# Fourth layer of a four-layer transformer kernel: the order of one division on VectorE, and the forget weights as 32 standing columns

## What is computed

```python
kvf = hs @ shared_w_kvf                       # hs: normed rows, 256 x 1024
k_sh = rms_norm(split_heads(kvf[..., :HD]), shared_k_norm_g)
f_logit = kvf[..., 2 * HD:] + shared_b_f      # 16 columns, one per head
f_cum = lax.cumsum(jax.nn.log_sigmoid(f_logit), axis=1).transpose(0, 2, 1)
q = rms_norm(split_heads(hn @ fox_w_q[j]), fox_q_norm_g[j])
...
logits = einsum('bhqd,bhkd->bhqk', qb, k) * scale + fb[..., :, None] - f_cum[:, :, None, :]
logits = jnp.where(causal, logits, -jnp.inf)
probs = jax.nn.softmax(logits, axis=-1)       # per tile of 128 queries
out = einsum('bhqk,bhkd->bhqd', probs, v)
```

## Time and profile before

| | before |
|---|---|
| median of 3 runs (lowest, highest) | 1344.83 us (1344.74, 1345.34) |
| the profiled execution's own time | 1345.62 us |
| its span, first to last instruction | 1343.5 us |
| PE busy, share of the span | 1327.1 us, 99% |
| PEld busy | 1104.4 us, 82% |
| DVE busy | 920.0 us, 68% |
| ACT busy | 779.2 us, 58% |
| POOL busy | 109.4 us, 8% |
| granted TensorE clock | 1.000 |
| HBM | 238.33 MB read, 178 GB/s over the span |

### The profile page before, as it was taken

How to read it: one execution, slowest core, us unless ns; L and a number is a source line. 1 busy time by engine, 2 the same in 40 slices (tenths; PEclk the granted TensorE clock), 3 DMA queues, 4 the chain that set the end, 5 groups by cost and what they waited for, 6 DMA issues and landing times.

```text
span 1343.5 us, 20709 instructions
## 1 busy us (share of the span) xinstructions
PE 1327.1 (99%) x6866; PEld 1104.4 (82%) x6866; DVE 920.0 (68%) x1612; ACT 779.2 (58%) x1415; POOL 109.4 (8%) x175
## 2 busy tenths in 40 slices
PE   8999999999999999999999999999999999999998
PEld 6987888888898788888888888888887778888887
DVE  6887665656787765555688875555677887655565
ACT  7666555546765655554675565555477766555544
POOL 4031232300000000000010000000002210000000
PEclk9999999999999999999999999999999999999999
DMA  8444777765554455555644455656645545655551
GB/s 315 150 157 134 213 221 219 219 205 182 181 165 142 146 183 187 187 187 187 213 140 152 131 172 188 187 187 187 203 157 181 167 133 164 195 187 187 187 200 51
DMA packets 144863, 240.32 MB, mean 179 GB/s; under 512 B 12643, under 2 KB 103314, under 8 KB 144801
## 3 DMA queue, kind: packets, MB, share of 16 engines
q1 hardware_dynamic: 141648, 230.41, 53.2%
q0 software_dynamic: 2832, 8.49, 3.2%
q10 hardware_dynamic: 320, 0.60, 0.1%
HBM read 238.33 MB, written 1.13 MB: 178 GB/s over the span
## 4 chain that ended last, share of the span: by engine, by line
PE 91%; DVE 5%; DMA 1%; ACT 1%; issue 1%; POOL 0%; SPq 0%; DVEq 0%
PE acc L1442 14%; PE acc L1444 14%; PE acc L1443 14%; PE sc L1444 11%; PE sc L1442 11%; PE sc L1443 11%; PE turn L1603 5%; PE acc L1553 3%; PE acc L1555 2%; PE acc L1554 2%; DVE wlo L1022 2%; PE turn L1690 1%; DMA raw<-in_qk 1%; PE sc L1650 1%; PE sc L1645 1%
## 5 line engine op out<-in xcount | busy, mean ns | idle before, releaser
L1022 DVE SCALAR_TENSOR_TENSOR wlo<-raw,gain,whi 128x512 fp32r<-128x512 f32 (+2 forms) x612 | 429.6, 756 | 26.3 <-ACT whi L735 26.3
L735 ACT ACTIVATE whi<-raw,gain 128x512 fp32r<-128x512 f32 (+2 forms) x612 | 404.5, 721 | 32.3 <-PE acc L1444 23.4
L1442 PE MATMUL sc<-whi,xhi 128*128 128x512 f32 x640 | 252.9, 395 | 0.0
L1444 PE MATMUL sc<-whi,xlo 128*128 128x512 f32 x640 | 249.7, 390 | 0.0
L1443 PE MATMUL sc<-wlo,xhi 128*128 128x512 f32 x640 | 249.3, 389 | 0.0
L1442 PE MATMUL acc<-whi,xhi 128*128 128x512 f32 x432 | 173.4, 401 | 3.2 <-DVE wlo L1033 1.8
L1444 PE MATMUL acc<-whi,xlo 128*128 128x512 f32 x432 | 168.7, 390 | 0.0
L1443 PE MATMUL acc<-wlo,xhi 128*128 128x512 f32 x432 | 168.4, 390 | 0.0
L1020 DVE TENSOR_TENSOR wlo<-raw,whi 128x1024 fp32r<-128x1024 f32 x120 | 141.8, 1217 | 0.0
L1444 PEld LDWEIGHTS sc<-whi,xlo 128*128 128x128 f32 x640 | 120.1, 188 | 25.6
L1443 PEld LDWEIGHTS sc<-wlo,xhi 128*128 128x128 f32 x640 | 120.3, 188 | 24.0
(11 more groups left out here) (194 smaller groups left out, 1992.3 us busy)
## 6 DMA issues: line engine op xcount, KB each, us to landing
raw<-in_ffn_w_gu SPq DMA_DIRECT2D x176, 256.0 KB
raw<-in_qk SPq DMA_DIRECT2D x62, 512.0 KB
raw<-in_ffn_w_gate SPq DMA_DIRECT2D x88, 256.0 KB
raw<-in_ffn_w_up SPq DMA_DIRECT2D x88, 256.0 KB
raw<-in_ffn_w_down SPq DMA_DIRECT2D x44, 512.0 KB
raw<-in_ffn_w_d SPq DMA_DIRECT2D x44, 512.0 KB
raw<-in_ple_w_gate SPq DMA_DIRECT2D x32, 512.0 KB
raw<-in_da_w_qkv SPq DMA_DIRECT2D x8, 512.0 KB
```

What stands on the lines that cost most here:

```text
L735: ins = act.activation(whi[:, u % RING, c0:c1], raw[:, u % RING, c0:c1], ACT.Copy, scale=scale)
L1022: ins = dve.scalar_tensor_tensor(out=lo, in0=w, scalar=gain[:, g:g + 1], in1=hi.bitcast(F32), op0=ALU.mult, op1=ALU.subtract)
L1442: pe.matmul(dst, xh, wh, start=first, stop=False)
L1444: return pe.matmul(dst, xl, wh, start=False, stop=last)
```

## The change

Two edits, both in the fourth layer.

1. In `DVE_STEPS` the entry r = 4 of L_FX is written the other way round: `post0`, the division of tile 0, comes ahead of `scores1`, the maxima of tile 1. It holds for each of the four groups.
2. `wfhi` and `wflo` lie side by side in one tensor, 32 columns for each block of 128. The matmuls high by high and low by high (standing low, moving high) are one matmul with 32 standing columns, so that 16 matmuls stand where 24 did; the result has 32 partitions, which are copied and turned together, and the two halves are added after the turn: DVE's four instructions of 128 x 8 become eight, with a `link` between the fourth and the fifth.

```diff
-    L_FX: [["evacqk"], ["headnorm"], ["evacv"], ["mask", "scores0"], ["scores1", "post0"], ["turnp0", "post1"], ["turnp1"],
+    L_FX: [["evacqk"], ["headnorm"], ["evacv"], ["mask", "scores0"], ["post0", "scores1"], ["turnp0", "post1"], ["turnp1"],
            ["pvt*"]],
...
-        wfhi = sb("wfhi", [P, KB, 16], F32R)
-        wflo = sb("wflo", [P, KB, 16], F32R)
+        wf_both = sb("wf_both", [P, KB, 2, 16], F32R)
+        wfhi, wflo = wf_both[:, :, 0, :], wf_both[:, :, 1, :]
...
-        fT, nfcT = o[0:16, 0, :], o[0:16, 1, :]
+        fT2, fT, nfcT = o[0:32, 0, :], o[0:16, 0, :], o[0:16, 1, :]
...
-                        dve.tensor_copy(fT, tb[e % 2][0:16, 0:S]).then_inc(turn_out[e % 2], 1)
+                        dve.tensor_copy(fT2, tb[e % 2][0:32, 0:S]).then_inc(turn_out[e % 2], 1)
...
-                        for t in range(T):
-                            for q in range(2):
-                                fd = f[:, t, :].rearrange("p (j q b) -> p q j b", q=2, b=2)[:, q]
-                                fs = tb[e % 2][:, 16 * t:16 * t + 16].rearrange("p (j q b) -> p q j b", q=2, b=2)[:, q]
-                                ins = dve.scalar_tensor_tensor(out=fd, in0=fs, scalar=rs(L, 0, t), in1=bp[:, q],
-                                                               op0=ALU.mult, op1=ALU.add)
+                        for part in range(2):
+                            for t in range(T):
+                                for q in range(2):
+                                    fd = f[:, t, :].rearrange("p (j q b) -> p q j b", q=2, b=2)[:, q]
+                                    fs = tb[e % 2][:, 32 * t + 16 * part:32 * t + 16 * part + 16]
+                                    ins = dve.scalar_tensor_tensor(out=fd, in0=fs.rearrange("p (j q b) -> p q j b", q=2,
+                                                                                            b=2)[:, q],
+                                                                   scalar=rs(L, 0, t), in1=fd if part else bp[:, q],
+                                                                   op0=ALU.mult, op1=ALU.add)
+                            if part == 0:
+                                link(ins)
...
                             for kb in range(KB):
-                                ins = three(tb[e % 2][0:16, 0:S], wfhi[:, kb, :], wflo[:, kb, :], xhi[:, kb, :],
-                                            xlo[:, kb, :], kb == 0, kb == KB - 1)
+                                pe.matmul(tb[e % 2][0:32, 0:S], wf_both[:, kb, :, :], xhi[:, kb, :], start=kb == 0,
+                                          stop=False)
+                                ins = pe.matmul(tb[e % 2][0:16, 0:S], wfhi[:, kb, :], xlo[:, kb, :], start=False,
+                                                stop=kb == KB - 1)
                             ins.then_inc(turned, 1)
...
-                            turn(e, [fT[:, t * P:(t + 1) * P] for t in range(T)])
+                            turn(e, [fT2[:, t * P:(t + 1) * P] for t in range(T)])
```

## The result

The changed kernel takes 1347.59 us (median of 17 runs, 1346.93 to 1349.22), the kernel before 1345.13 (17 runs, 1344.66 to 1346.16): a ratio of 1.0017, 95% interval 1.0011 to 1.0024. That is 2.5 us slower, a small loss within the 0.2% that the prediction set as its bound. The forecast was 1347.2, a loss of 2.4 us, and the time lies in its range, 1345.2 to 1348.7.

The account below looks back on a forecast made before the run. PE, with work in 99% of the span, bounds the kernel. Edit 2's -0.29 and edit 1's -0.16, +0.86, +0.88 and +1.07 sum to +2.36, on the median 1344.83 giving 1347.2 us; range 1345.2 to 1348.7.

Parts of the forecast that it names:

- Edit 2: Forget gates: matmuls 0.95 us earlier, DVE's additions cost 0.66, so -0.29 at the wait for `qkv`; bounds -0.95 and +0.34.
- The wait that swallowed the rest: PE's waits at 1025 to 1026 us, ahead of group 0's scores, get longer by 0.6 us.
- The rule of the Trainium skill: Forget matmuls: a weight load grows with its columns, 13 ns more for 32 than 16; if exposed, edit 2 saves 0.1 less.
- Edit 1, group 0: Division of tile 0 fits DVE's idle time; the chain to `turnqk1` comes 0.16 us earlier: -0.16, bounds 0 and -0.6.
- The maxima stay where they are: Group 0: the division, done at 1036.94, fits DVE's idle time until 1037.12, so tile 1's maxima do not move.
- Edit 1, groups 1 to 3: Maxima 1.27, 1.29, 1.48 us later, less 0.41 slack at `turnp1`: +0.86, +0.88, +1.07, added up.
- Nothing there: Groups 1 to 3: DVE's lateness reaches no further, neither to `wlo` nor to `qkv` of groups 2 and 3.
- 1 us and more: Sign: a new wait of PE at `turnp1` for tile 1's division in each of groups 1 to 3, this long.
- The sum: Whole kernel: -0.29 - 0.16 + 0.86 + 0.88 + 1.07 = +2.36 us, a small loss just within 0.2%.
- the wait goes and none takes its place: Rival at `turnp0` and `turnp1`: no new wait replaces the removed one; 1342.0, rather 1343 us; chance 0.06.
- Absorption: Rival, groups 1 to 3: part of the delay is caught up, half of 2.81 left, 1345.8 us; chance 0.20.
- POOL's roots: Rival, groups 0 and 1: two roots lengthen by 0.38 each, +0.76, 1348.0 us, past the 0.2%; chance 0.12.

Follow-up runs that it names:

- e1_order_only: Kernel before with the new DVE order alone, in all four groups, forget gates as before; 1347.83 us against 1345.36, ratio 1.002.
- e3_group0: Changed kernel with the division first in group 0 alone, groups 1 to 3 in the old order; 1344.62 us against 1345.36, ratio 0.9996.
- e2_forget_only: Changed kernel with the old DVE order, so edit 2 alone; 1344.64 us against 1345.36, ratio 0.9995.
- e10_t0_oldorder: Changed kernel without edit 1, two halves summed in PE's turn, `turnp0` in the middle of its unit; 1344.13 us against 1345.21, ratio 0.9989.
- e11_t0_pad5: e10_t0_oldorder with five tiny DVE memsets added in the third layer; 1344.01 us against 1345.24 for the kernel before, ratio 0.9992.
- e4_turnp1_mid: Changed kernel with PE's `turnp1` moved to the middle of its unit, six matmuls later; 1345.83 us against 1345.36 for the kernel before, ratio 1.0004.
- e5_groups123: Kernel before with the division first in groups 1 to 3 alone, forget gates as before; one run, 1347.88 us against 1345.12.

## Why the prediction was right, point by point

- **Edit 2.** The matmuls start the gates' chain 0.97 earlier (forecast 0.95), DVE's additions cost 0.66 (0.66), and PE's wait for `qkv` comes 0.30 earlier (0.29). Right up to that wait; by the yardstick edit 2 alone gave 0.62, and its other 0.3 was not forecast. The wait that swallowed the rest, forecast at 0.6 for 1025 to 1026, is one place earlier, at the transposes of `o` (0.73 us). The load of 32 columns takes 108 ns, that of 16 takes 94 (the rows by tile above): 14 more, and hidden, since the blocks are spaced by 0.23 for two matmuls. The rule of the Trainium skill cited for this ("TensorE: Matmul & The Clock Gate", "LDWEIGHTS (loading the stationary operand)") gives 13 and agrees; exposed it was not.
- **Edit 1, group 0.** Forecast -0.16. Measured -0.34 alone (e1_order_only), and +0.02 on top of edit 2 (e3_group0 against e2_forget_only). The step that failed is "The maxima stay where they are". I had taken the 1.73 us of DVE's idle time for PE's scores, to the last bit, but 0.37 of it was not PE's. Starts in us after the first forget matmul:

  | kernel | maxima | ACT's last reading of tile 1 | product of tile 1 | ACT's squares | `ss_h` | `turnqk1` |
  |---|---|---|---|---|---|---|
  | before | 27.22 | 31.01 | 31.60 | 31.58 | 32.74 | 39.02 |
  | e1_order_only | 27.04 | 30.82 | 31.25 | 31.40 | 32.40 | 38.68 |
  | e2_forget_only | 26.56 | 30.35 | 30.94 | 30.93 | 32.09 | 38.36 |
  | e3_group0 | 26.74 | 30.52 | 30.95 | 31.10 | 32.10 | 38.38 |
  | e10_t0_oldorder | 26.59 | 30.37 | 30.96 | 31.33 | 32.11 | 38.39 |
  | e11_t0_pad5 | 26.21 | 30.00 | 30.59 | 31.32 | 31.95 | 38.23 |

  The forecast's own 0.16 is there: with the division first the product of tile 1 starts 0.43 behind ACT's reading instead of 0.59, in e1_order_only and in e3_group0. What the forecast lacked is the shift of the maxima, which the rest of the chain follows. With the division first they start at its end, 1.04 behind ACT's reading. On the code of before that is 0.18 earlier than the old start, 0.34 in all; on the code of edit 2 it is 0.18 later than the old start, and the two cancel. From e10_t0_oldorder to e11_t0_pad5 the maxima come 0.38 earlier and `ss_h` only 0.16: there it follows ACT's squares, which have not moved, as they stand behind ACT's copy of PE's later `turnp0`. In the changed kernel `turnqk1` is 0.63 earlier than before, and the forecast had 0.45; but behind `qkv` the gain of 0.33 is the unforeseen shift of edit 2, not edit 1. That this term came out near was luck.
- **Edit 1, groups 1 to 3.** Forecast +0.86, +0.88, +1.07, in all +2.81. Counted from the first forget matmul PE goes on behind `turnp1` 0.23, 1.13 and 2.22 later than before (1063.84 against 1064.53, 1087.48 against 1087.27, 1111.13 against 1109.83); with the 0.63 gained until then, that is +0.86, +0.90 and +1.09, and +2.87 up to `h`. The steps: maxima 1.29 later in group 1 (forecast 1.27), product to turn 1.29 (1061.70 to 1062.99; 1.29), turn to next matmul 0.85 (0.84). The step "Nothing there", on how far DVE's lateness reaches, did this sum no harm, but of the kernel it is wrong: e4_turnp1_mid shows 0.84. The matmuls' waits of 0.97 and 0.98 in groups 2 and 3 are a shade under the "1 us and more" that I wrote; only group 1 has more, 1.33.
- **The sum.** +2.24 by the yardstick, +2.46 by the medians, +2.36 forecast. The errors are 0.17 in group 0 and 0.06 in groups 1 to 3, smaller than what the times can tell. The terms of the two edits are less right than their sum: forecast -0.29 and +2.65, measured by the yardstick -0.62 for edit 2 and then +2.86 for edit 1.
- **The rivals.** That the wait goes and none takes its place is refuted by the three waits at `turnp1`. It would have gained less, too: the matmuls saw 0.8 of the 2.5 (0.42 less than the weight loads in groups 0 and 1, not 0.2), which gives 1343.7 and not 1343. Absorption: none, the delay arrives in full; e3_group0 and e5_groups123 place it. POOL's roots: the long root occurred again, once, and at the same place as before, so no chain got longer by it:

```profile
1022.50 0.68 DVE L1337 TENSOR_TENSOR_SCAN o<-ones_sb,o 16x256 f32<-16x256 f32 x1
1022.59 2.03 POOL L609 TENSOR_TENSOR r_h<-r_h,powm 128x8 f32<-128x8 f32 x1
```

## What to carry to other kernels

A wait of the bounding engine names the instruction that is late, not the instruction to hurry. Look at who stands behind it in the same queue: here putting the division first delayed ten instructions by 1.3 us, whose consumer had 0.41 of slack, while moving the waiting turn back on PE removed the same wait at a price of 0.22 in group 0 and none that shows in the others. Where an order pays in one group of a loop and costs in the others, as an idle gap exists only in the first, let the table say so for each group (here group 0's order gained 0.40, 0.16 or nothing, by the code around it); and check a promised gain of tenths against a kernel that only shifts the code.

## What was not expected of the hardware

- The start of DVE's maxima behind the same scores took 1.66 us in before and 1.29 with 4, 5 or 11 instructions more ahead of it in DVE's program, none of which runs within 10 us. By the yardstick that is 0.37 us of the kernel, more than edit 2 itself (0.25 to 0.31). It repeats to 0.01 in a program, and no wait names it: the trace puts the whole idle time down to PE (1.73, and 1.35 with 5 memsets), though DVE's semaphore wait starts 1.19 us behind the scores in both. It stays at one place of DVE's program, and a packet of instructions goes with it; that the loading of instructions causes it is not shown.
- A root of 128 x 8 on POOL takes 1.64 to 1.66 us and 2.03 where DVE's scan begins ahead of it and `qkv` follows (the rows above; 2.04 in before). This was so in all fourteen traces: once 2.03 or 2.04, else 1.64 to 1.66. The second root of group 1 also has a `qkv` beside it, for 0.27 us in before, and took 1.64; the scan runs beside no other root of 128 x 8. That points to the scan, but no run takes it away.
- Two fp32 matmuls of 32 x 16 take 0.31 us longer, from PE's start to DVE's, than two transposes by the identity of 32 columns (0.72 and 0.41). They have four rows in the trace, the transposes two.
